# Rope's swaps on GpSimd, earlier evictions, an earlier sum matmul and spread-out coefficients in a two-layer hybrid decoder

## What is computed

```python
def hybrid_layer(h, ...):
    xn = rms_norm(h, norm_g)
    proj = xn @ w_in
    qa, fa, ia, ga, qb, kb, vb, gb, uc, gc = split(proj)
    oa = hgrn2_mixer(qa, fa, ia, lb, valid)          # 4 heads, gated linear recurrence
    ya = rms_norm(oa, hgrn_norm_g)
    qh = rope(rms_norm(qb, q_norm_g), pos)           # 16 heads of 64
    kh = rope(rms_norm(kb, k_norm_g), pos)           # 2 heads of 64
    yb = swa_sink_attention(qh, kh, vb, sinks)       # window 128, meta tokens visible
    yc = multiscale_pool(uc, valid, pool_w, pool_scale)
    return h + concat(ya * silu(ga), yb * silu(gb), yc * silu(gc)) @ w_out

def rope(x, pos):
    x1, x2 = x[..., :half], x[..., half:]
    return concat([x1 * cos - x2 * sin, x2 * cos + x1 * sin])
```

## Time and profile before

| | |
|---|---|
| time, median of 3 runs | 1599.99 us (1599.67 to 1600.09) |
| profiled execution | 1600.59 us, span 1598.8 us |
| mean granted clock of TensorE | 0.996 |
| TensorE busy | 1566.5 us, 98% |
| VectorE busy | 912.7 us, 57% |
| ScalarE busy | 671.5 us, 42% |
| GpSimd busy | 172.5 us, 11% |
| DMA | 151.70 MB, 95 GB/s in the mean |

### The profile page before, as it was taken

The page is one execution under the profiler, slowest core; times in us unless marked ns, Lnnn a source line. Parts: engine busy times, 40 slices in busy tenths (PEclk is TensorE's granted clock), DMA queues, the critical chain, the costliest instruction groups (busy, mean ns, idle before and its releaser), DMA issues.

```text
span 1598.8 us, 26797 instructions
## 1 busy us (share of the span) xinstructions
PE 1566.5 (98%) x10736; PEld 1442.6 (90%) x10736; DVE 912.7 (57%) x1738; ACT 671.5 (42%) x1322; POOL 172.5 (11%) x312
## 2 busy tenths in 40 slices
PE   8889999999999999999999999999999999999999
PEld 8889999999999999999998889888999878888887
DVE  6677687766666554433335776776676565443231
ACT  6668566622222432323226775665132333222121
POOL 0000565400000000000000006543000000000000
PEclk9999999999999999999999999999999999999999
DMA  7222211123211222434433221121331212334342
GB/s 270 74 77 80 80 54 54 54 81 107 72 63 53 84 102 87 146 128 140 140 123 107 79 90 70 54 80 53 92 94 54 80 55 103 102 110 156 124 157 66
DMA packets 39020, 151.70 MB, mean 95 GB/s; under 512 B 5345, under 2 KB 14065, under 8 KB 23921
## 3 DMA queue, kind: packets, MB, share of 16 engines
q1 hardware_dynamic: 38464, 149.42, 27.6%
q10 hardware_dynamic: 432, 0.57, 0.1%
HBM read 141.13 MB, written 8.59 MB: 94 GB/s over the span
## 4 chain that ended last, share of the span: by engine, by line
PE 90%; DVE 5%; issue 2%; ACT 1%; POOL 1%; DMA 1%; SPq 0%; DVEq 0%; POOLq 0%; ACTq 0%
PE ps_gemm L1058 77%; PE ps_mix L977 3%; PE ps_mix L899 2%; PE ps_mix L945 2%; PE ps_mix L913 1%; PE ps_gemm L860 1%; PE ps_gemm L847 1%; PE ps_mix L1021 1%; DMA x_in<-in_xT 1%; PE ps_mix L847 1%; PE ps_mix L941 1%; PE ps_mix L1023 0%; POOL w_lo L514 0%; DVE w_lo L1130 0%; PE ps_mix L972 0%
## 5 line engine op out<-in xcount | busy, mean ns | idle before, releaser
L1058 PE MATMUL ps_gemm<-x_hi,w_hi 128*128 128x264 f32 (+1 forms) x2176 | 546.6, 316 | 6.9 <-DVE z L1234 6.4
L1058 PE MATMUL ps_gemm<-x_hi,w_lo 128*128 128x264 f32 (+1 forms) x2176 | 529.6, 308 | 0.0
L1058 PE MATMUL ps_gemm<-x_lo,w_hi 128*128 128x264 f32 (+1 forms) x2176 | 529.0, 308 | 0.0
L1058 PEld LDWEIGHTS ps_gemm<-x_hi,w_hi 128*128 128x128 f32 x2176 | 353.9, 190 | 27.3 <-DVE z L1234 6.8
L1058 PEld LDWEIGHTS ps_gemm<-x_hi,w_lo 128*128 128x128 f32 x2176 | 353.6, 189 | 19.4
L1058 PEld LDWEIGHTS ps_gemm<-x_lo,w_hi 128*128 128x128 f32 x2176 | 352.9, 189 | 16.6
L599 ACT ACTIVATE w_hi<-w_stage 128x512 fp32r<-128x512 f32 x464 | 266.9, 619 | 166.2 <-DVE z L1218 122.7
L1130 DVE TENSOR_TENSOR w_lo<-w_stage,w_hi 128x512 fp32r<-128x512 f32 x392 | 257.4, 689 | 91.9 <-ACT w_hi L599 81.7
L1058 PE MATMUL ps_gemm<-mixed_hi,w_lo 128*128 128x264 f32 (+1 forms) x768 | 205.2, 322 | 0.0
L1058 PE MATMUL ps_gemm<-mixed_lo,w_hi 128*128 128x264 f32 (+1 forms) x768 | 205.0, 321 | 0.0
L1058 PE MATMUL ps_gemm<-mixed_hi,w_hi 128*128 128x264 f32 (+1 forms) x768 | 203.8, 320 | 0.0
(11 more groups left out here) (185 smaller groups left out, 1601.0 us busy)
## 6 DMA issues: line engine op xcount, KB each, us to landing
w_stage<-in_w_in SPq DMA_DIRECT2D x82, 1024.0 KB, 4.8
w_stage<-in_w_out SPq DMA_DIRECT2D x32, 1024.0 KB, 5.2
res<-in_xT SPq DMA_DIRECT2D x16, 264.0 KB, 5.2
h1T<-z SPq DMA_DIRECT2D x16, 264.0 KB, 5.6
res<-h1T SPq DMA_DIRECT2D x16, 264.0 KB, 5.2
a_rden<-rden SPq DMA_DIRECT2D x32, 128.0 KB, 4.8
out<-z SPq DMA_DIRECT2D x16, 256.0 KB, 5.5
x_in<-in_xT SPq DMA_DIRECT2D x3, 1056.0 KB, 13.0
```

The source lines that it names most:

```text
L1058: ins = pe.matmul(g[:, bank, 0:size], ws, xs[:, k, c:c + size], start=tick == 0 and i == 0, stop=tick == TICKS - 1 and i == 2)
```

## The change

In layer 0's rope stage, and in both layers for the swaps:

- The two swap copies leave ScalarE and go to GpSimd, at step 0 of each rope, with the same waits (for the eviction and for the end of the rope before). They write `tb` as before.
- The sum matmul of layer 0's ropes comes after step 5 of the rope instead of step 8, and Ln and Exp at step 6 instead of 9. In layer 1 they stay.
- Evictions in layer 0: block 2 at step 58 (before: 62), block 3 at 71 (72), block 4 at 84 (the same), block 5 at 96, the rule's place (98).
- The four level mask copies go one by one to step 13 of blocks 4 to 7. The negated sinks and the first four coefficient operations go to block 8, step 13, the next three to block 9, step 13, and the last eight, four for each layer, to step 14 of blocks 9 and 10.

```diff
-ROPE_LAST = (13, 17)
-LATE_OUT = {0: 3 * TICKS + 6, 1: 3 * TICKS + 6, 2: 62, 3: 72, 4: 84, 5: 98}, {0: 1 * TICKS + 12}
+ROPE_MINI, ROPE_LAST = (5, 8), (13, 17)
+LATE_OUT = {0: 3 * TICKS + 6, 1: 3 * TICKS + 6, 2: 58, 3: 71, 4: 84, 5: 96}, {0: 1 * TICKS + 12}
...
+            def rope_swap(layer, n):
+
+                R = NROPE * layer + ROPE_CHUNKS.index(n)
+                zi = (NC * layer + n) % 2
+                c0, w = span(layer, n)
+                pool.wait_ge(s_z, NC * layer + n + 1)
+                if R:
+                    pool.wait_ge(s_ropeo, R)
+                for quarter in range(2):
+                    a, b = 32 * quarter, 32 * (quarter ^ 1)
+                    pool.tensor_copy(tb[a:a + 32, PAD + c0:PAD + c0 + 2 * w],
+                                     z[b:b + 32, zi, PAD + c0:PAD + c0 + 2 * w]).then_inc(s_swap, 1)
+
             for N in range(NTOT):
                 layer, n = divmod(N, NC)
                 for tick in range(TICKS):
+                    r = rope_at(layer, n, tick, 0)
+                    if r is not None:
+                        rope_swap(layer, r + 1)
                     if 1 <= tick <= 4 and n and CHUNKS[n - 1][0] == "u":
                         pooling(N - 1, tick - 1)
...
                         act.activation(sqh[:, cols], zz[:, cols], ACT.Square).then_inc(s_sqh, 1)
-
-                        for quarter in range(2):
-                            a, b = 32 * quarter, 32 * (quarter ^ 1)
-                            act.activation(tb[a:a + 32, PAD + c0:PAD + c0 + 2 * w],
-                                           z[b:b + 32, zi, PAD + c0:PAD + c0 + 2 * w], ACT.Copy)\
-                               .then_inc(s_swap, 1)
...
-                    r = rope_at(layer, n, tick, MINI_TICK + 1)
+                    r = rope_at(layer, n, tick, ROPE_MINI[layer] + 1)
...
-                    r = rope_at(layer, n, tick, MINI_TICK)
+                    r = rope_at(layer, n, tick, ROPE_MINI[layer])
                     if r is not None:
                         mini(N, layer, 2 + r)
...
-                    if N == 5 and tick == 7:
-                        level_masks()
-                    if N == 6 and tick == 7:
-                        hgrn_coefficients()
+                    if N in (4, 5, 6, 7) and tick == 13:
+                        level_mask(N - 4)
+                    if N == 8 and tick == 13:
+                        lower_bounds()
+                    if N == 9 and tick == 13:
+                        lower_bound_sums()
+                    if N in (9, 10) and tick == 14:
+                        hgrn_coefficients(N - 9)
```

More of the change, by code:

```diff
@@ L1180, in lb_differences, with level_mask, lower_bounds @@
                 dve.tensor_tensor(lbt[:, 1], l1, lbt[:, 4], ALU.subtract).then_inc(s_lb, 1)
-            def level_masks():
-                for b in range(4):
-                    link(dve.tensor_copy(lmask[:, :, b], lmask_f[:]))
-            def hgrn_coefficients():
+            def level_mask(b):
+                link(dve.tensor_copy(lmask[:, :, b], lmask_f[:]))
+            def lower_bounds():
                 link(dve.tensor_scalar(nsink[:], prm_sb[:, :, C_SINK:C_SINK + HB], -1.0, None, ALU.mult))
@@ L1194, in hgrn_coefficients, with lower_bound_sums @@
                 link(dve.tensor_tensor(lbt[:, 3], lbt[:, 3], lbt[:, 5], ALU.mult))
+            def lower_bound_sums():
                 link(dve.tensor_tensor(lbt[:, 6], lbt[:, 2], lbt[:, 2], ALU.subtract))
@@ L1197, in hgrn_coefficients @@
                 link(dve.tensor_tensor(lbt[:, 7], lbt[:, 7], lbt[:, 2], ALU.subtract))
-                for layer in range(DEPTH):
-                    lb, (a, b, na, ha) = lbt[:, 6 + layer], (coef[:, layer, i] for i in range(4))
-                    link(dve.tensor_scalar(a, lb, -0.5, 0.5, ALU.mult, ALU.add))
-                    link(dve.tensor_tensor(b, lb, a, ALU.add))
-                    link(dve.tensor_scalar(na, a, -0.5, None, ALU.mult))
-                    link(dve.tensor_scalar(ha, a, 0.5, None, ALU.mult))
+            def hgrn_coefficients(layer):
+                lb, (a, b, na, ha) = lbt[:, 6 + layer], (coef[:, layer, i] for i in range(4))
+                link(dve.tensor_scalar(a, lb, -0.5, 0.5, ALU.mult, ALU.add))
+                link(dve.tensor_tensor(b, lb, a, ALU.add))
+                link(dve.tensor_scalar(na, a, -0.5, None, ALU.mult))
+                link(dve.tensor_scalar(ha, a, 0.5, None, ALU.mult))
             def take_out(N):
```

## The result

The changed kernel takes 1590.24 us in the median of four executions (1589.19 to 1590.87), the kernel before 1599.83 us beside it: a ratio of 0.994 with a 95% interval of 0.9922 to 0.9957. The gain is 9.6 us, where 13.5 were forecast, and the time lies 0.24 us outside the range.

The account below looks back on a forecast made before the run. TensorE, busy 98% of the span, was taken to bound the kernel. Losses of 16.7 us before and 2.0 + 0.8 + 0.4 = 3.2 after gave 13.5 us gained: 1586.5 us against the median of 1599.99, range 1583.6 to 1590.0.

Parts of the forecast that it names:

- The gain is kept: After step 130 every engine stands to TensorE as before, so the 13.5 us gained lasts to the end.
- The stalls before: Layer 0's rope stage, steps 57 to 130 of the kernel before: 16.7 us lost to stalls and low clock.
- The first stall: Rope 0's sum matmul waits for square_lo until about 58.5 us: 2.0 us instead of 5.85; block 4 has no wait.
- Rival 1: TensorE's clock falls in the 2.0 us stall at rope 0, costing 1.6 to 3.0 us: 1588.1 to 1589.5; 15%.
- The walk: Every instruction of three queues followed in written order, giving by how much each rope's square_lo comes ahead of TensorE.
- Rope 4: Its square_lo is done at 99.2 us, TensorE has issued step 113 at 98.4: short by 0.8 us.
- the 0.4 for interference: GpSimd's swaps slow one VectorE w_lo in rope 0's path and one in rope 4's: 0.4 us together, bounds nothing to 1.
- Rope 7: Its square_lo comes ahead of TensorE by 0.5 us, so no stall there.
- rival 2: Thin margins of ropes 1, 2, 7 and 8 are eaten, each ending in a stall: 1 to 4 us, 1587.5 to 1590.5; 11%.
- the 3.2 us allowed for all stalls left: Losses left in the rope stage after the change: 2.0 at rope 0, 0.8 at rope 4, 0.4 for interference.
- The swaps on GpSimd: A pair taken at 2.2 us, costing nothing up to 1.8 us each; first-call loading, estimated at 0.4 us, left out.
- Masks and coefficients: 2.58 and 3.2 us moved to blocks 4 to 10, within VectorE's spare 1.5 us per rope, except rope 4's mask.

Follow-up runs that it names:

- a3_sum_step8: The changed kernel with the sum matmul of layer 0's ropes back at step 8, all else as changed; 1585.79 us.
- b1_coef_old: The changed kernel with level masks and coefficients back at their old steps (blocks 5 and 6, step 7); 1590.65 us.
- c3_sum_alone: The kernel before with only the sum matmul of layer 0's ropes moved to step 5; 1598.15 us.
- c1_swap_behind_square: The changed kernel with GpSimd's swaps held until square_lo of the same rope is done; 1590.20 us.
- d1_changed: One of three more traced executions of the changed kernel, no edit; the three took 1589.96, 1589.76 and 1589.15 us.

## Why the prediction was off

Two steps failed. In the stage, the margins behind rope 4 were too wide, and rope 7 stalled where 0.5 us of margin had been worked out; with the rest of the stage this makes 1.3 us of the miss. The larger one stands in the last line of the sum, "against the median of 1599.99, 1586.5 us": a gain worked out in one trace is taken to the median of other executions one to one. That is 1.7 to 2.6 us, for which the sum had no term. "The gain is kept" holds where the clock doesn't fall: behind the stage the traces then take 1443.0 and 1443.1 us before and 1442.9 after.

**The stalls before: right.** 16.7 us were said to be lost from step 57 on; a3_sum_step8, the same work without a stall, puts it at 16.3.

**The first stall: right.** 2.0 us said, 1.69 with the 0.16 of overhang, so 1.85, found. ScalarE's weight quarter began at 55.04 us, 1.47 us sooner against the stage's start where 1.34 were worked out, block 4 had no wait, and the clock stayed up. Rival 1 did not happen. The walk also had the next ropes right: the margins of ropes 1 to 3 were given as 0.65, 0.7 and 1.9 us and are 0.8, 0.8 and 1.9.

**Rope 4: the place right, the size short.** 0.8 us and part of the 0.4 for interference were forecast, 1.22 (1.4 with the overhang) found. square_lo itself took 1.07 us there. I had charged the interference to a w_lo at 0.2 us, about half of the 0.36 to 0.43 that it is, and only in two ropes.

**Rope 7: the step that failed in the stage.** "Square_lo comes ahead of TensorE by 0.5 us" there was the thinnest but one of my margins, and I charged no interference to it. square_lo took 1.14 us, and TensorE waited 0.41 (0.57 with the overhang). From rope 4 on the error grows: margins of 2.2 and 2.8 us were forecast for ropes 5 and 6 and 1.8 and 2.2 are found, and square_lo is stretched in exactly the ropes 4 to 7. With the swaps held the wait at rope 7 is gone. Two more things stand in this path. Rope 6 is no rope of 8.5 us on VectorE: from its square_lo to rope 7's it takes 12.66 us, more than the period of 9.99, because the split of k's second half and the weight quarter behind it stand there. And the negated sinks and first four coefficient operations, which the change puts at block 8, step 13, stand there as well, for 1.0 us. VectorE in the changed kernel, the first of them, the eviction behind the last, and rope 7's square_lo:

```profile
126.35 0.17 DVE L1198 TENSOR_SCALAR neg_sinks<-prm_sb 128x32 f32<-128x32 f32 x1
...
127.36 0.71 DVE L1248 TENSOR_TENSOR z<-ps_gemm,rstd 128x528 f32<-128x528 f32 x1
...
130.12 1.14 DVE L1163 TENSOR_TENSOR square_lo<-ta,square_hi 128x528 fp32r<-128x528 f32 x1 [0.58 <-ACT square_hi L691]
```

In b1_coef_old, with the coefficients elsewhere, the same stretch takes 11.63 us and rope 7 doesn't wait (TensorE, too, comes later there, after the longer stall at rope 4). Placing these five operations one rope earlier was not run. The stall is rival 2, in one rope of the four named; rope 8 lost another 0.1. "From step 130 on neither kernel has a stall" was therefore wrong, too. Of the 3.2 us allowed for all stalls left, 4.1 came. With the 0.4 us too much at the start of the sum (16.7 against 16.3), that makes 12.2 where 13.5 stood.

**From the stage to the time: not costed at all.** The rest of the miss, 1.7 to 2.6 us (12.2 less the 10.5 and 9.6 us measured), is more than all errors in the stage. I took the gain of one trace to the median one to one. But the trace of before was one with an early start (32.89 us; 32.96 to 34.36 in all others) and no fall of the clock in the HGRN stages, and the changed kernel's traces have a start 0.2 to 1.1 us later and, in three of five, a fall of 1.5 us. That accounts for the traces: none of the five took the 1588.4 us that 12.2 less than 1600.59 would be. It doesn't account for the kernel before, whose executions beside the first result all took less than its trace, 1599.50 to 1600.09 us. The shortest execution of the kernel before, 1599.45 us at a span of 1597.7, leaves at most 121.9 us for the stage if it started no sooner and took no less behind the stage than any trace (32.89 and 1442.9 us). So the 122.8 us of both traces are not every execution's, and part of the rest lies in the stage of the kernel before, where the clock falls twice. How much, no run shows. My range's width came from the stalls of one stage alone. It should have held a term of 1 to 2 us for what differs between executions; the kernel before itself later ran from 1599.45 to 1602.03 us. With the errors of the stage alone the time would have been 1587.8, well inside the range.

**The sum matmul: a part I never priced.** I counted its sooner Exp as help and its sooner demand only inside the walk of the whole. The runs give its price: 4.3 us lost in the changed kernel (a3_sum_step8), 2.2 us won on the kernel before (c3_sum_alone). It helps where VectorE is held up behind Exp and TensorE stalls later for it. In the kernel before that is rope 0: its Exp ends at 69.1 us, the weight quarter stands behind it on ScalarE, and VectorE waits for the quarter. With the sum alone at step 5 it doesn't. VectorE in the kernel before, then in c3_sum_alone:

```profile
69.73 0.69 DVE L1130 TENSOR_TENSOR w_lo<-w_stage,w_hi 128x512 fp32r<-128x512 f32 x1 [5.94 <-ACT w_hi L599]
```

```profile
65.29 0.69 DVE L1130 TENSOR_TENSOR w_lo<-w_stage,w_hi 128x512 fp32r<-128x512 f32 x1
```

There the two waits of ropes 2 and 3 go, and the second fall of the clock costs 1.2 us less (11.77 us against 12.96 for a sum and 13 steps), while rope 7 loses 0.3.

In the changed kernel nobody stalls for want of Exp in rope 0, and the sooner sum costs on two sides. TensorE asks for square_lo 2.2 us earlier, with margins of under 1 us in most ropes. And Ln and Exp of rope 3, now due at step 101, stand ahead of the split of k's first half (step 103) and the weight quarter behind it (step 104) in ScalarE's order; with the sum at step 8 they are due at step 104 and stand behind both. VectorE then waits for that quarter, and square_lo of rope 4 starts 65.67 us into the stage, against 62.98 in a3_sum_step8. VectorE in the changed kernel, then in a3_sum_step8:

```profile
94.91 0.69 DVE L1140 TENSOR_TENSOR w_lo<-w_stage,w_hi 128x512 fp32r<-128x512 f32 x1 [2.73 <-ACT w_hi L615]
```

```profile
91.07 1.29 DVE L1140 TENSOR_TENSOR w_lo<-w_stage,w_hi 128x512 fp32r<-128x512 f32 x2
```

**The swaps on GpSimd: right in kind, their price dearer than needed.** 1.30 to 1.82 us a pair against 2.2 taken; VectorE's timeline shows no wait for them; they start 0.03 us behind the squares already in rope 0 (53.98 against 53.95), and the first pair takes 1.82 us, so first use has no price of that size here, and the estimate by the Trainium skill's 6 us for a first call (GPSIMD Engine Reference, Instruction dispatch) is not borne out. The Trainium skill's rule on shared SBUF interfaces (GPSIMD Engine Reference, Key points) is: c1_swap_behind_square, set against the changed kernel, shows that the swaps are what lengthens square_lo, which has two SBUF inputs, by 0.43 us, and in the changed kernel a pair of swaps beside it takes 0.45 us more than one alone.

**Masks and coefficients: hidden for the most part.** At their new places all of them cost nothing in a3_sum_step8, which has no stall. In the changed kernel the one mask is in rope 4's path, as said, but the coefficients in rope 6 aren't in VectorE's spare time, as said under rope 7. What spreading them out is worth depends on the company: 0.6 us by the medians (2.2 by the stage) in the changed kernel, where rope 4 stalls anyway, and 3.1 us (4.3 by the stage) where nothing else stalls.

## What to carry to other kernels

An engine that must meet a date in another one's order is helped by an earlier input and hurt by an earlier date; an operation that is moved sooner can be both, and it also passes other work in the order of the engine behind it, so it is worth running the change with that move alone undone. Stalls in one chain are not a sum: take one away and look at the margin of the next date, since what is under that margin comes back there. And a gain worked out from one trace needs a term for what differs between executions, here a start within 1.5 us and falls of TensorE's clock at 1.5 us each, beside the bounds of the change itself.

## What the hardware showed that I had not expected

- TensorE's clock can fall behind a wait of 1.8 to 2.0 us between well filled stretches, in some executions and not in others of the same program: 1.00 throughout in two of five traces of the changed kernel (but for its very end), under 1.00 near 400 or 1190 us in three, one of which (`d1_changed`) also had 0.57 at 8 to 12 us. Each fall near 400 or 1190 us cost about 1.5 us. No fall came in the 1.69 us wait at 59 us in five traces; in c3_sum_alone one came behind a wait of 2.42 us.
- A copy on GpSimd and a subtraction with two SBUF inputs on VectorE slow each other down: 0.71 to 1.14 us for the subtraction, 1.30 to 1.76 us for the pair of copies. A pair of VectorE's own copies of 32 partitions goes from 0.89 to as much as 1.52 us beside them, and the swaps to 1.84.
- GpSimd copies 32x528 float32 in 0.65 us when alone (1.30 for a pair), as fast as ScalarE (1.31 for a pair).
